# Two products of RWKV's block inverse with 64 stationary columns, and a layer norm step placed first in its slot

## What is computed

```python
def rwkv7_mixer(hn, mu, w_in, w_out, w0, ..., v_first, vres):
    ...
    def step(state, inp):
        r_t, w_t, k_t, v_t, kk_t, a_t = inp
        sk = jnp.einsum('bhvk,bhk->bhv', state, kk_t)
        state = state * w_t[:, :, None, :] - sk[..., None] * (kk_t * a_t)[:, :, None, :] + v_t[..., None] * k_t[:, :, None, :]
        return state, jnp.einsum('bhvk,bhk->bhv', state, r_t)
    ...
    y = head_norm(y, LNX_EPS) * lnx_g + lnx_b
    ...
```

## Time and profile before

| | us |
|---|---|
| median of three runs | 3797.18 |
| lowest and highest | 3791.0, 3809.89 |
| the profiled execution | 3782.67 |
| its span, first to last instruction | 3781.1 |
| TensorE, matmuls, busy | 3539.1 (94%) |
| TensorE, weight loads, busy | 2914.3 (77%) |
| VectorE busy | 2063.2 (55%) |
| ScalarE busy | 1691.4 (45%) |
| GpSimd busy | 125.4 (3%) |
| mean granted TensorE clock | 0.954 |

### The profile page before, as it was taken

One profiled execution on the slowest core, in us unless ns is written; L12 is line 12 of the kernel. 1 busy time (PEld: TensorE's weight loads), 2 busy tenths in 40 slices (PEclk: granted clock), 3 DMA queues, 4 the chain that ended last, 5 costly groups with the idle time before them and its releaser, 6 DMA issues. The chain is left out here.

```text
span 3781.1 us, 47824 instructions
## 1 busy us (share of the span) xinstructions
PE 3539.1 (94%) x18546; PEld 2914.3 (77%) x18546; DVE 2063.2 (55%) x4012; ACT 1691.4 (45%) x3185; POOL 125.4 (3%) x126
## 2 busy tenths in 40 slices
PE   7999898989998899998899899999789999999799
PEld 6888647868876677777787688888668888888687
DVE  3144333364335677877434467777745566665552
ACT  3222462264442444443314556656632665665431
POOL 0011120000001000000000000000100000000000
PEclk9999999989998888989899899999889999999899
DMA  4333403112232212212221111111122211110321
GB/s 142 124 132 108 158 1 134 40 62 89 100 104 63 70 46 54 70 46 45 93 92 56 55 29 45 35 35 35 51 100 78 88 36 40 40 40 12 134 73 45
DMA packets 219337, 264.54 MB, mean 70 GB/s; under 512 B 62700, under 2 KB 142692, under 8 KB 218088
## 3 DMA queue, kind: packets, MB, share of 16 engines
q1 hardware_dynamic: 219112, 261.48, 21.6%
HBM read 191.43 MB, written 69.99 MB: 69 GB/s over the span
## 5 line engine op out<-in xcount | busy, mean ns | idle before, releaser
L332 PE MATMUL bank<-wh,XH 128*128 128x512 f32 x1344 | 535.8, 399 | 24.6 <-DVE wl L316 19.6
L332 PE MATMUL bank<-wl,XH 128*128 128x512 f32 x1344 | 528.5, 393 | 0.0
L332 PE MATMUL bank<-wh,XL 128*128 128x512 f32 x1344 | 528.5, 393 | 0.0
L2633 PE MATMUL bank<-XH,wh 128*128 128x512 f32 x1040 | 424.9, 409 | 10.1 <-DVE wl L2622 9.6
L2633 PE MATMUL bank<-XH,wl 128*128 128x512 f32 x1040 | 409.1, 393 | 0.0
L2633 PE MATMUL bank<-XL,wh 128*128 128x512 f32 x1040 | 408.4, 393 | 0.0
L332 PEld LDWEIGHTS bank<-wh,XH 128*128 128x128 f32 x1344 | 256.3, 191 | 79.0 <-DVE wl L316 14.0
L332 PEld LDWEIGHTS bank<-wl,XH 128*128 128x128 f32 x1344 | 255.4, 190 | 54.4
L332 PEld LDWEIGHTS bank<-wh,XL 128*128 128x128 f32 x1344 | 256.2, 191 | 51.1
L316 DVE TENSOR_TENSOR wl<-raw,wh 128x1024 fp32r<-128x1024 f32 x128 | 157.0, 1237 | 249.9 <-ACT wh L307 248.6
L332 PE MATMUL bank<-XH,wh 128*128 128x512 f32 x704 | 280.6, 399 | 8.0 <-DVE XL L1585 8.0
(11 more groups left out here) (416 smaller groups left out, 6991.0 us busy)
## 6 DMA issues: line engine op xcount, KB each, us to landing
sc_zt<-stage SPq DMA_DIRECT2D x88, 256.0 KB, 2.0
raw<-in_att_w_in SPq DMA_DIRECT2D x33, 512.0 KB, 4.2
raw<-in_even_w_in SPq DMA_DIRECT2D x32, 512.0 KB, 5.2
raw<-in_odd_w_in SPq DMA_DIRECT2D x32, 512.0 KB, 4.8
raw<-in_rec_w_in SPq DMA_DIRECT2D x32, 512.0 KB, 4.0
sc_h<-H SPq DMA_DIRECT2D x24, 512.0 KB, 2.6
sc_z<-stage SPq DMA_DIRECT2D x40, 256.0 KB, 2.0
z<-sc_z SPq DMA_DIRECT2D x8, 1024.0 KB, 5.8
```

Of the source, the lines that this page charges most:

```text
L332: done = e.matmul(out, lhsT, rhs, start=k == 0 and j == 0, stop=k == NK - 1 and j == 2)
L2633: done = e.matmul(bank[:, :], x[:, k, :], y[:, k, ts], start=k == 0 and j == 0, stop=k == NK - 1 and j == 2)
```

## The change

Two edits, which don't touch each other:
- In the block inverse the tile `X` shrinks from 128 to 64 columns for each of its four systems: its two blocks are now stored side by side (columns 0 to 31 and 32 to 63). H loads these 64 columns, and of `TT` only the second and the fourth block of 32 columns move, 64 columns in place of 128; the results stand in 64 partitions and 64 columns a system, and ScalarE's two copies read them there. Y loads 64 columns of `NT` (64 to 127) in place of 128, and writes the upper 64 partitions alone, those that ScalarE copies. The number of products, of copies and of waits stays the same, and so do the copies' sizes.
- In `PLACED`, slot 11, `tail` 0, 0 comes first, ahead of `lora` 1, the scan and three rows of the solve.

```diff
--- before.py
+++ after.py
@@ -1720,7 +1720,7 @@
     8: ((2, 'lora', 0), (1, 'solve', 3)),
     9: ((1, 'solve', 4),),
     10: ((2, 'keys'), (1, 'solve', 2)),
-    11: ((2, 'lora', 1), (2, 'scan'), (1, 'solve', 3), (0, 'tail', 0, 0)),
+    11: ((0, "tail", 0, 0), (2, 'lora', 1), (2, 'scan'), (1, 'solve', 3)),
     12: ((1, 'solve', 4),),
     13: ((0, 'tail', 0, 1), (1, 'solve', 2)),
     14: ((2, 'norm'), (0, 'tail', 0, 2), (1, 'solve', 3)),
@@ -1848,7 +1848,7 @@
         self.be, self.ka = [be0, c.sb("bet1", [P, S])], [ka0, c.sb("kap1", [P, S])]
         self.g, self.bv = c.sb("gf", [P, S]), [bv0, c.sb("bv1", [P, S])]
         self.mask3 = c.sb("mask3", [P, 3, P])
-        self.X, self.Y = c.sb("X", [P, 4, P]), c.sb("Y", [P, 4, 64])
+        self.X, self.Y = c.sb("X", [P, 4, 64]), c.sb("Y", [P, 4, 64])
         self.M, self.KBV = c.sbs("mk", [P, 2, 3 * P], 2), c.sbs("kbv", [P, 3, P], 2)
         self.R, self.U, self.S, self.SG = c.sb("R", [P, P]), c.sb("U", [P, P]), c.sbs("S", [P, P], 2), c.sb("SG", [P, P])
         self.yc, self.sq, self.zo = c.sb("yc", [P, 512]), c.sb("sq", [P, 512]), c.sbs("zo", [P, 512], 2)
@@ -2150,12 +2150,14 @@
                 done = e.matmul(b2[0:64, 32 * i:32 * i + 32], TT[:, 4 * g + i, 0:64], self.X[:, i, 0:32], start=True, stop=True)
             done.then_inc(*self.prod.up("G", p, g))
             for i in range(4):
-                done = e.matmul(b1[:, self.chunk(i)], self.X[:, i, :], TT[:, 4 * g + i, :], start=True, stop=True)
+                odd = TT[:, 4 * g + i, :].rearrange("p (q a) -> p q a", a=32)[:, 1:4:2, :]
+                done = e.matmul(b1[0:64, 64 * i:64 * i + 64], self.X[:, i, :], odd, start=True, stop=True)
             part = "H"
         elif part == "Y":
             e.wait_ge(*self.level.at("G", p, g))
             for i in range(4):
-                done = e.matmul(b2[:, P + 64 * i:P + 64 * i + 64], NT[0:64, 4 * g + i, :], T[0:64, 4 * g + i, 0:64], start=True, stop=True)
+                done = e.matmul(b2[64:128, P + 64 * i:P + 64 * i + 64], NT[0:64, 4 * g + i, 64:128], T[0:64, 4 * g + i, 0:64],
+                                start=True, stop=True)
         else:
             e.wait_ge(*self.level.at("Y", p, g))
             e.wait_ge(*self.level.at("H", p, g))
@@ -2322,13 +2324,13 @@
                 e.wait_ge(*self.zeros.at("X"))
             e.wait_ge(*self.prod.at("X", p, g))
             e.activation(self.X[r[1], :, 0:32], four(b1, r[1], 0, 32, P), ACT.Copy)
-            e.activation(self.X[r[3], :, 64:96], four(b1, r[3], 0, 32, P, 64), ACT.Copy).then_inc(*self.level.up("X", p, g))
+            e.activation(self.X[r[3], :, 32:64], four(b1, r[3], 0, 32, P, 64), ACT.Copy).then_inc(*self.level.up("X", p, g))
         elif part == "G":
             e.wait_ge(*self.prod.at("G", p, g))
             e.activation(self.T[x][r[1], gs, 0:32], four(b2, r[1], 0, 32, 32), ACT.Copy).then_inc(*self.level.up("G", p, g))
             e.wait_ge(*self.prod.at("H", p, g))
-            e.activation(self.TT[x][r[0], gs, 32:64], four(b1, r[0], 0, 32, P, 32), ACT.Copy)
-            e.activation(self.TT[x][r[2], gs, 96:128], four(b1, r[2], 0, 32, P, 96), ACT.Copy).then_inc(*self.level.up("H", p, g))
+            e.activation(self.TT[x][r[0], gs, 32:64], four(b1, r[0], 0, 32, 64), ACT.Copy)
+            e.activation(self.TT[x][r[2], gs, 96:128], four(b1, r[1], 0, 32, 64, 32), ACT.Copy).then_inc(*self.level.up("H", p, g))
         elif part == "Y":
             e.wait_ge(*self.prod.at("Y", p, g))
             e.activation(self.Y[64:128, :, :], four(b2, slice(64, 128), P, 64, 64), ACT.Copy).then_inc(*self.level.up("Y", p, g))
```

## The result

| | before | after |
|---|---|---|
| median, us (of four, run on one chip) | 3794.09 | 3740.0 |
| lowest and highest | 3787.06, 3809.89 | 3736.31, 3745.34 |
| the profiled execution, and its span | 3782.67, 3781.1 | 3741.03, 3739.4 |
| mean granted clock | 0.954 | 0.953 |

The ratio of the times is 0.987 (0.9832 to 0.9908). Two later comparisons, on other chips, gave 0.9888 (0.9856 to 0.9921) and 0.9889 (0.9867 to 0.991). Over 68 executions of the kernel before, in all later comparisons, the mean is 3784.7 us, over all 14 of the changed kernel 3742.5: it is 42 us faster, 1.1%, and part of the 54 us between the first medians is the scatter of the four executions of before. The forecast was 22 us. The busy times of the page answer to the earlier trace rows: 34 us less of matmuls, 26 of weight loads, nothing on VectorE.

The account below looks back on a forecast made before the run. TensorE, busy 94% of the span, was taken to bound the kernel. Its part, 13.6 us, plus 8.6 for the tail's step made 22.2 us, from a median of 3797.2 to 3775.0; range of 8 in 10: 3761 to 3794.

Parts of the forecast that it names:

- What bounds the kernel: In each pair TensorE leads to slot 10, VectorE from slot 11's scan to the solve's end, then ScalarE a few us.
- Narrower sets, 0.85 us a group: Inverse groups: G and H together save 0.41 us, Y 0.44; 27.2 us over 32 groups as upper bound.
- Group 0's little: Group 0: savings end in waits for ScalarE's `T` and `R`, so only 0.16 us a pair in p = 1 to 6.
- The tail's step, 8.6 us: Slot 11: the 1.54 us step fills VectorE's wait for `lw`; 6.2 us in p = 2 to 5, 2.4 in 0 and 1.
- No new wait of a microsecond for product y in slot 11: VectorE, slot 11: product y is there before `lw`; a new wait of a microsecond or more would show the prediction wrong.
- I take no change as the likeliest: Granted clock, all pairs: where it falls hangs on small shifts, so the sum gives it nothing.
- The clock takes some of it: Rival: less H and Y work in group 2 makes the clock fall in p = 0, 1, 3 too; 3786 us, chance 0.14.
- The clock gains too: Rival: without the `yc` wait p = 0 and 1 keep full clock, 4 us less each; 3767 us, chance 0.12.
- Slower: Rival: TensorE stays at the lower clock from `lora` to the next pair, 4.5 to 6.0 us each; 3800 us, chance 0.07.
- One of my signs of being wrong: Profile after, any pair: its granted clock moving by more than 0.05 either way would show the prediction wrong.
- Pair 7: Last pair, to its last product u: 3.5 us less, with 1.5 from group 0 and 0.7 from group 3.

Follow-up runs that it names:

- e7: Kernel before, with Y keeping 128 stationary columns and streaming its 64 moving columns twice, no work removed: ratio 1.0005 to the kernel before.
- e1: Kernel before with only the tail's first step moved to the head of slot 11: ratio 0.9967 to the kernel before.
- e3: Kernel before with only H narrowed, to 64 stationary and 64 moving columns: ratio 1.0022 to the kernel before.
- e10: Kernel before with H's stationary columns narrowed to 64 and all 128 columns still moving: ratio 0.9972 to the kernel before.
- e2: Kernel before with H and Y narrowed and the tail's step left where it was: ratio 0.9943 to the kernel before.
- e4: Kernel before with only Y narrowed, to 64 stationary columns: ratio 0.9948 to the kernel before.
- e5: Kernel before with Y narrowed and the tail's step first, H as before: ratio 0.989 to the kernel before.
- e6: Changed kernel with H moving all 128 columns past its 64 stationary ones: ratio 0.9868 to the kernel before.
- e8: Changed kernel without its two unread products in slots 12 and 15: 3753.2 us, ratio 0.9912 to the kernel before.
- e9: e6 with G streaming 64 columns in place of 32, the second half unread: ratio 0.9867 to the kernel before.
- e12: e6 again, beside the changed kernel on one chip: 3734.31 us, ratio 0.9868 to the kernel before.
- e13: e6 with two more unread products ahead of X of group 0, where TensorE waits for the DMA: 3750.01 us, ratio 0.9914 to the kernel before.
- e11: Kernel before with the tail's step first and Y streaming its 64 columns twice past 128 stationary ones: ratio 0.994 to the kernel before.

## Why the prediction was wrong

The forecast was 22 us and 3775; the first comparison gave 3740.0, below the range, and all executions together 42 us. By its steps:

- **What bounds the kernel**, three parts of a pair and who leads in each: right, and it explains the result. A lower clock costs time where TensorE leads (b), and nothing where VectorE does (e), but the second holds only once the tail's step is first: e then takes 17.0 us in every pair of every profile, with 0 to 10.1 us of lower clock in it. Without that it takes 18.5 us, and up to 21.0 with 13.7 us of it (e7).
- **Narrower sets, 0.85 us a group**: about right. By medians over the 32 groups, from a set's first load to the next set's first, G goes from 0.58 to 0.46 us, H from 1.09 to 0.61, Y from 1.03 to 0.61: G and H together 1.07 (forecast 1.06), all three 1.02 less. Pairs at full clock up to the solve (p = 2, 4, 5 of both first profiles) take 31.9 to 32.0 us for a where they took 33.0 to 33.4: 1.0 to 1.4 a pair, forecast 1.01. **Group 0's little** was right too (0.17 for 0.16 us in p = 4).
- **The tail's step, 8.6 us**: right. Alone it gives 9.3 at equal low-clock time. In the traces it is 6 x 1.54 = 9.2 us of e; the other 1.6 is a wait of VectorE's for `nr` in p = 0 and 1 that I had not seen. It stands where e has 10 us of lower clock or more, as in p = 2 and 4 of e7, so it is a price of the clock that goes with the earlier step. In p = 0 of before:

```profile
1306.81 0.17 DVE L2418 TENSOR_SCALAR nr<-nr 128x16 f32<-128x16 f32 x1 [1.17 <-ACT nr L2296]
```

- **No new wait of a microsecond for product y in slot 11**: right at the full clock (0.04 us). With the lower clock it exists (1.16 us in e1), but `lw` is later still.
- **"I take no change as the likeliest"**, of the clock, is the step that failed. The sum had nothing for it, and in b it was worth 13.8 us: b lost 16.4 us where the sum had 2.6. In the first profile three falls make 4.5, 4.5 and 4.9 of it (20.5, 20.5 and 20.9 us against the 16.0 of p = 3, without one). The rows for it were there: the stretch's length with a fall and without, and a fall just behind Y's first load, the product that the change narrows. I had read the fall of p = 4 as coming after the `lora` products; it comes between Y and F, ahead of the second of them. And I took its place for chance ("hangs on small shifts"). It isn't: in all five profiles whose Y has 128 stationary and 64 moving columns (before twice, e1, e3, e10) it is there in three to five pairs of six, 17 falls in all, each 0.9 to 1.9 us behind Y's first load; in the eleven with 64 and 64 (the changed kernel three times, e2, e4, e5, e6, e8, e9, e12, e13) and the two with 128 and 128 (e7, e11) no pair is lengthened by it. That it isn't Y's length, e7 shows, whose Y is as long. What it is beyond that stays open, and so does why the lower clock then turns up elsewhere.
- **Where that gain went.** a gave 4.0 us less than forecast and f took 3.1: the lower clock that left b is partly there, 17 and 15 us more than before. So the clock's term is +13.8 in b and -7.1 in a and f, 6.7 net. With it, 1.6 in e and 5.0 in pair 7 that are mostly chance, the profiles give 35.6 us. The 42 of the timed executions are some 6 more, because the profiles of before are of short executions: 3782.67 and 3774.04 us, 6.4 under the mean of 68 and with 30 us less at the lower clock, where the three of the changed kernel lie at their mean. Which places that time would be in isn't shown (single profiles of one kernel lie up to 21 us apart in row a).
- **"The clock takes some of it"** (3786): the mechanism exists, but not through the group's work as such. H with half its moving columns has more time at the lower level wherever the two forms were compared (433 us in e3 for 347 in e10; 347 in the changed kernel for 293 to 301 in e6 and e12).
- **"The clock gains too"** (3767): right sign, wrong place. I put it in p = 0 and 1, from the wait for `yc` that goes. The wait went, in all pairs; the fall stayed, in p = 1 for 17.1 us from 1371.9 us on.
- **"Slower"** (3800): in the first profile the clock does stay low up to the next pair, in five of six pairs. It costs 3 us in f each time (10.1 to 10.5 for 6.8 to 7.9) and nothing in e; I had priced it at 4.5 to 6.0. One of my signs of being wrong came with it: the granted clock of pair 3 moved by more than 0.05, from 0.96 to 0.83.
- **Pair 7**, -8.5 us where 3.5 was forecast: one profile of before, with 30.7 us of lower clock there, carries it.

A rule cited before the result, that idle waits send TensorE to its half clock (the Trainium skill, "TensorE: Matmul & The Clock Gate", HAM oscillation), doesn't explain this fall: ahead of it TensorE was busy, by its matmul rows, for 9.43 us of 9.82, and e7, with the same 9.43, has no fall. e13 filled a wait and lost by it; e8, which took work out of waits, lost as that rule says. The other one, that a change of tiling mode drains the engine (the Trainium skill, "TensorEngine Tiling (Array Packing)", Key Properties), agrees with the step from G to H, both in one mode now: 0.46 us for 0.59.

## What to carry over

Where two engines take turns in leading a loop, ask of a throttled clock where in the loop it falls, not how much of it there is: a fall of 13.7 us, 10.6 of them ahead of the scan, cost 4.5 us there, and 10 us of lower clock between the scan and the end of the solve cost nothing once the tail's step was first. A fall that comes behind the same product in several pairs of every profile belongs to the kernel, and a twin that changes only that product's moving side and removes nothing shows it. But look at the whole time too: in e7 that fall was gone and nothing was gained. Shorter products may not be worth their length: with 64 moving columns in H and not 128 the kernel was 0.5% slower beside the old Y (e3, e10), and the fastest kernel here gives H its 128 moving columns back.

## What I had not expected of the hardware

- Halving H's moving columns, with 64 stationary either way, went with a mean of 433 us at the lower clock for 347 beside the old Y, and of 347 for 293 to 301 beside the narrow one.
- Doubling Y's moving columns from 64 to 128, with 128 stationary, cost next to nothing: eight loads span 0.96 us either way, and the next set begins 1.09 us behind the first of them for 1.03 (medians).
- In fp32, a set of eight loads with 64 stationary columns takes 0.61 us to the next set with 64 columns moving and 1.02 with 128 (H in e6), against 1.09 with 128 by 128: the shorter load shows only where the moving side is short too.
- A us at the lower clock costs 0.31 us on the whole, and by its place between nothing (in e, with the tail's step first) and 0.4 to 0.5 (4.5 to 4.9 us for 10.6 to 11.5 us of it in b; 3.2 us for 6.8 in a of the changed kernel).
